# Norm factor after the projections: value tiles first, all projection tiles from unnormalised x, in a two-layer decoder trunk

## The reference

```python
def rms_norm(x, g):
    return x * rsqrt(mean(x * x, axis=-1, keepdims=True) + NORM_EPS) * g

def rope(x, pos):                      # on the first 16 of 64 channels of a head
    x1, x2 = x[..., :half], x[..., half:ROT_DIM]
    return concat([x1 * cos - x2 * sin, x2 * cos + x1 * sin, x[..., ROT_DIM:]])

h = rms_norm(x, norm_g) @ w_in         # one projection; split into q, k, v, gates ...
q_a, k_a, q_c, k_slc, k_win = rope(...)    # v and the raw rows of the compressed branch: no rope
x = x + merge_branches(p, o_a, o_b, o_c, w_up_a, w_up_b, w_up_c, w_out)
...
y = rms_norm(x, final_norm_g)
```

## Time and profile before

| | before |
|---|---|
| median of 3 runs | 1014.2 us (1012.84 to 1017.59) |
| profiled execution | 1013.01 us, of which the span of instructions is 1011.3 us |
| granted TensorE clock, mean over the span | 0.995 of full speed |
| PE busy | 948.9 us, 94% |
| DVE / ACT / POOL busy | 59% / 42% / 18% |
| HBM | 200.12 MB read, 40.18 MB written |

### The profile page before, as it was taken

How to read it: one execution, slowest core, us unless ns; L and a number is a source line. 1 busy time by engine, 2 the same in 40 slices (tenths; PEclk the granted TensorE clock), 3 DMA queues, 4 the chain that set the end, 5 groups by cost and what they waited for, 6 DMA issues and landing times. The chain is left out here.

```text
span 1011.3 us, 20944 instructions
## 1 busy us (share of the span) xinstructions
PE 948.9 (94%) x7828; PEld 864.0 (85%) x7836; DVE 597.5 (59%) x1305; ACT 424.3 (42%) x837; POOL 185.6 (18%) x320
## 2 busy tenths in 40 slices
PE   4999999998999999999999999999889999999995
PEld 4999887887778689999999998878777777999994
DVE  5868766557222357746686786665742234676564
ACT  5453345544312244334454434545432205443343
POOL 3010000126436620000000000003463464000000
PEclk9999999999999999999999999999999999999998
DMA  9563964536658881532645576636346699434421
GB/s 344 210 224 133 412 237 187 229 116 208 231 157 254 258 324 53 223 141 92 252 184 212 230 284 277 249 127 244 146 153 207 214 257 306 192 126 157 176 84 48
DMA packets 65189, 206.30 MB, mean 204 GB/s; under 512 B 12080, under 2 KB 49648, under 8 KB 55744
## 3 DMA queue, kind: packets, MB, share of 16 engines
q1 hardware_dynamic: 56048, 184.72, 49.3%
q0 software_dynamic: 8752, 19.63, 6.4%
q10 hardware_dynamic: 288, 0.60, 0.2%
HBM read 200.12 MB, written 40.18 MB: 238 GB/s over the span
## 5 line engine op out<-in xcount | busy, mean ns | idle before, releaser
L952 PE MATMUL bank<-xnT_high_r,paged_r 128*128 128x288 f32 x1088 | 327.7, 301 | 4.0 <-DVE oT_a L1687 2.4
L952 PE MATMUL bank<-xnT_r,paged_r 128*128 128x288 f32 x1024 | 302.7, 296 | 0.0
L952 PE MATMUL bank<-xnT_high_r,big_r 128*128 128x288 f32 x1024 | 301.8, 295 | 0.0
L1598 DVE TENSOR_TENSOR big_r<-big,paged_r 128x1024 fp32r<-128x1024 f32 x160 | 194.4, 1224 | 135.1 <-ACT paged_r L1399 134.4
L952 PEld LDWEIGHTS bank<-xnT_high_r,paged_r 128*128 128x128 f32 x1088 | 204.7, 188 | 11.6 <-issue 5.1
L952 PEld LDWEIGHTS bank<-xnT_high_r,big_r 128*128 128x128 f32 x1024 | 193.4, 189 | 0.0
L952 PEld LDWEIGHTS bank<-xnT_r,paged_r 128*128 128x128 f32 x1024 | 193.1, 189 | 0.0
L1399 ACT ACTIVATE paged_r<-big 128x1024 fp32r<-128x1024 f32 x160 | 166.4, 1050 | 7.4 <-DMA big<-in_w_feat 4.1
L1145 PE MATMUL bank<-paged,long 128*128 128x256 f32 x512 | 117.6, 383 | 2.1 <-DVE kvp L1773 1.7
L1145 PEld LDWEIGHTS bank<-paged,long 128*128 128x128 f32 x512 | 94.8, 190 | 19.8 <-issue 4.5
L922 POOL TENSOR_SCALAR short<-short,small 128x128 f32<-128x128 f32 (+1 forms) x64 | 50.6, 805 | 321.0 <-DVE small L1747 321.0
(11 more groups left out here) (294 smaller groups left out, 1473.7 us busy)
## 6 DMA issues: line engine op xcount, KB each, us to landing
big<-in_w_tok SPq DMA_DIRECT2D x13, 2048.0 KB, 8.5
big<-in_w_feat SPq DMA_DIRECT2D x12, 2048.0 KB, 8.6
big<-in_w_gate SPq DMA_DIRECT2D x10, 2048.0 KB, 8.6
out_kept_dil<-in_cache_dil SPq DMA_DIRECT2D x16, 1020.0 KB, 13.3
paged<-in_pool SPq DMA_DIRECT2D x218, 64.0 KB, 3.0
big<-in_w_up SPq DMA_DIRECT2D x12, 1024.0 KB, 8.8
paged<-in_pool POOLq DMA_DIRECT2D x166, 64.0 KB, 2.9
big<-in_kv_win SPq DMA_DIRECT2D x4, 2048.0 KB, 9.3
```

What stands on the lines that cost most here:

```text
L952: last = mm(out, l, r, start=(c == 0 and i == 0), stop=(c == n - 1 and i == 2))
L1598: v.tensor_tensor(l_part, full, h_part.bitcast(FP32), ALU.subtract).then_inc(*split_done.inc(s))
```

## The change

- The value tiles are projected first, then the keys; all 28 tiles read the unnormalised `xg`, so `RAW` and `pout` go. ACT evacuates all but the two cmp tiles, which DVE multiplies by `rnB`.
- The norm factor enters in three ways: in the rotation tables (`rots`: two DVE products of 128x288 into `rot_n`) for queries and keys, per token in the evacuation of the value transposes, and in `rnB` for the rest.
- `root` is now six PE products of one column, ones as the moving side, which leave the sum of squares as a column per token; ACT takes the square root of 128x3, DVE the reciprocal, and scales three pieces of the identity by it; `spread` multiplies ones by these diagonals, which gives the factor on every partition, and ACT copies it to `rnB`. In layer 0 `root` stands behind tile 3 and `spread` behind tile 4; in layer 1 behind tiles 0 and 1.
- Normalised x is still made, for the gate logits and the feature tiles; `norm` and `nlow` stand three tiles after `spread`, the last two chunks at tiles 13 to 15.
- The four value transposes move behind `gc`, and the rope of query type 3 (branch C) is split into two halves, on DVE behind the scaling of units 0 and 1. The zc feature tiles come before the za ones.
- In layer 0 the squares and their sums are POOL's, not ACT's and DVE's, and POOL's late constants are loaded behind them. ACT runs a square root on an unused tile at the head of each layer's start.
- The loads of the start: x in four parts, all on SP's queue, in the order x0, x1, w0, x2, x3, w1 to w3, constants, small loads.
- At the end the squares are made before the scaled x, the last square goes to PE unsummed, and `y` reads the factor from PSUM.

```diff
-TILES = [("k", t) for t in KEYED[0:4]] + [("v", t) for t in ("d1", "d4", "d16", "win")] + \
+TILES = [("v", t) for t in ("d1", "d4", "d16", "win")] + [("k", t) for t in KEYED[0:4]] + \
         [("k", "slc"), ("cmp", 0), ("cmp", 1), ("v", "slc")] + [("q", t, r) for t in range(4) for r in range(REP)]
 V_SLC = TILES.index(("v", "slc"))
-RAW = 8
-
-ROPES = {TILES.index(("k", "win")): ("k", 0), TILES.index(("k", "slc")): ("k", 1)} | \
+K_FIRST, K_SLC = TILES.index(("k", "d1")), TILES.index(("k", "slc"))
+
+ROPES = {TILES.index(("k", "win")): ("k", 0), K_SLC: ("k", 1)} | \
...
-FEATS = [("za", kt) for kt in range(WT)] + [("zc", kt) for kt in range(WT)] + \
+FEATS = [("zc", kt) for kt in range(WT)] + [("za", kt) for kt in range(WT)] + \
...
-        if i == 0:
-            out += [("root",), ("pout", 0)]
-        elif i == 1:
-            out += [("pout", 1), ("norm", 0), ("norm", 1)]
-        elif i == 2:
-            out += [("nlow", 0), ("nlow", 1), ("pout", 2), ("rnt",), ("norm", 2), ("norm", 3)]
-        elif i == 3:
-            out += [("nlow", 2), ("nlow", 3), ("pout", 3), ("norm", 4), ("norm", 5)]
-        elif i == 4:
-            out += [("nlow", 4), ("nlow", 5), ("norm", 6), ("norm", 7)]
-        elif i == 5:
-            out += [("nlow", 6), ("nlow", 7)]
-        elif i < 12:
+        root, first = (0, 1) if layer else (3, 4)
+        if i == root:
+            out.append(("root",))
+        elif i == first:
+            out += [("spread",), ("rots",), ("norm", 0), ("norm", 1)]
+        elif first < i < first + 3:
+            n = 2 * (i - first)
+            out += [("nlow", n - 2), ("nlow", n - 1), ("norm", n), ("norm", n + 1)]
+        elif i == first + 3:
+            out += [("nlow", 4), ("nlow", 5)]
+        elif 12 < i < 16:
+            out += [("nlow", z) for z in range(6, KT) if z == i - 8] + [("norm", z) for z in range(6, KT) if z == i - 7]
+        if i < 12:
...
+        if i in ROPES and ROPES[i] != ("q", 3):
             out.append(("rope",) + ROPES[i])
         if i == TILES.index(("cmp", 1)):
             out.append(("pairs",))
-        if RAW < i <= RAW + 3:
-            out.append(("vturn", i - RAW))
-        if i == V_SLC + 2:
-            out.append(("vturn", 0))
-    out += [("gc",), ("gct",)]
+    out += [("gc",)] + [("vturn", j) for j in range(4)] + [("gct",)]
...
+        if i < 2:
+            out.append(("rope", "q", 3, i))
...
-    out = start(0, 0) + halves(0, 0) + [s for i in range(1, KT) for s in start(0, i)] + halves(0, 1)
+    starts = [start(0, i) for i in range(KT)]
+    out = sum(starts[0:4], []) + halves(0, 0) + sum(starts[4:], []) + halves(0, 1)
...
-            out += [(layer, ("down", i // 4, i % 4))] + start(layer + 1, i)
+            out += [(layer, ("down", i // 4, i % 4))] + start(layer + 1, i)[::-1 if layer + 1 == DEPTH else 1]
...
-    return out + [(DEPTH, ("root",))] + [(DEPTH, ("y", i)) for i in range(KT // 2)]
+    return out + [(DEPTH, ("root",)), (DEPTH, ("spread",))] + [(DEPTH, ("y", i)) for i in range(KT // 2)]
...
+            load_x(0)
+            load_x(1)
+            load_first(0)
+            load_x(2)
+            load_x(3)
+            for q in range(1, 4):
+                load_first(q)
...
+                if k == "square" and layer == 0:
+                    i = s[1]
+                    pool.wait_ge(x_in[i // 2], 16)
+                    own = total[:, 0:T] if i == 0 else squared_x[i % 2][:, 0:T]
+                    done = nc.gpsimd.tensor_tensor(own, x[:, i, :], x[:, i, :], ALU.mult)
+                    if i == 0:
+                        done.then_inc(*summed.inc(s))
+                    elif i < KT - 1:
+                        link(done)
+                        pool.wait_ge(*summed.at(("square", i - 1)))
+                        nc.gpsimd.tensor_tensor(total[:, 0:T], total[:, 0:T], own, ALU.add).then_inc(*summed.inc(s))
+                    else:
+                        done.then_inc(*squared.inc(s))
+                        for dst, src in LATE:
+                            pool.dma_start(dst, src).then_inc(late_in, 16)
+                        numbers = page_numbers(pool, 0)
...
-                    pe.wait_ge(*summed.at(("square", KT - 1)))
-                    pe.wait_ge(set_up, 4)
+                    pe.wait_ge(*summed.at(("square", KT - 2)))
+                    pe.wait_ge(set_up, 6)
                     wait(pe, TR.is_free(s))
-                    mm(tr(s)[:, 0:T], ones[:, :], total, start=True, stop=True).then_inc(*TR.fill(s))
-                elif k == "rnt":
+                    for n, part in enumerate((total, squared_x[(KT - 1) % 2])):
+                        if n:
+                            pe.wait_ge(*squared.at(("square", KT - 1)))
+                        for tt in range(3):
+                            last = mm(tr(s)[:, tt:tt + 1], part[:, P * tt:P * (tt + 1)], ones[:, 0:1],
+                                      start=(n == 0 and tt == 0), stop=(n == 1), skip_group_check=True)
+                    last.then_inc(*TR.fill(s))
+                elif k == "spread":
                     pe.wait_ge(*inverted.at(("root",)))
                     pe.wait_ge(const_in, 16 * len(CONSTS))
-                    transposes(s, [(tr(s)[0:PARTS[tt], tt:tt + 1], rnB[0:1, TOK0[tt]:TOK0[tt] + PARTS[tt]])
-                                   for tt in range(3)])
+                    wait(pe, TR.is_free(s))
+                    for tt, n in enumerate(PARTS):
+                        last = mm(tr(s)[:, P * tt:P * tt + n], ones[0:n, :], diag[0:n, P * tt:P * tt + n],
+                                  start=True, stop=True, skip_group_check=True)
+                    last.then_inc(*TR.fill(s))
...
+                    precise(pj(s)[:, 0:T], lambda c: (wh[:, c, :], wl[:, c, :]),
+                            lambda c: (xg_high[:, c, :], xg_low[:, c, :]), KT, ("tok", g), q4,
+                            lambda c: x_split.at(("start", c))).then_inc(*PJ.fill(s))
                 elif k == "gc":
                     wait(pe, PJ.is_free(s))
                     pe.wait_ge(*layer_in.at("all"))
+                    pe.wait_ge(*xn_split.at(KT - 1))
...
+                    if i == 0:
+                        f(unused[:, layer:layer + 1], eps, ACT.Sqrt)
...
                 elif k == "root":
                     act.wait_ge(*TR.is_full(s))
-                    f(rnB, tr(s)[:, 0:T], ACT.Sqrt, bias=eps).then_inc(*TR.release(s))
-                elif k == "rnt":
+                    f(rn, tr(s)[:, 0:3], ACT.Sqrt, bias=eps, scale=1.0 / D_MODEL).then_inc(*TR.release(s))
+                elif k == "spread" and layer < DEPTH:
                     act.wait_ge(*TR.is_full(s))
-                    f(rn[:, 0:2], tr(s)[:, 0:2], ACT.Copy)
-                    f(rn[0:NS, 2:3], tr(s)[0:NS, 2:3], ACT.Copy).then_inc(*TR.release(s))
+                    f(rnB, tr(s)[:, 0:T], ACT.Copy).then_inc(*TR.release(s))
...
-                        f(v_prompt[:, :, slc], tr(s)[:, 0:2 * P].rearrange("p (t n) -> p t n", t=2), ACT.Copy)
-                        f(v_new[:, slc], tr(s)[0:NS, 2 * P:3 * P], ACT.Copy).then_inc(*TR.release(s))
+                        for tt, n in enumerate(PARTS):
+                            last = f(v_prompt[:, tt, slc] if tt < 2 else v_new[:, slc], tr(s)[0:n, P * tt:P * (tt + 1)],
+                                     ACT.Identity, scale=rn[0:n, tt:tt + 1])
+                        last.then_inc(*TR.release(s))
...
-                    v.reciprocal(rnB, rnB).then_inc(*inverted.inc(s))
-                    dve.wait_ge(*inverted.at(s))
-                elif k == "pout":
-                    dve.wait_ge(*PJ.is_full(("proj", s[1])))
-                    v.tensor_tensor(raw[0][:, s[1], :], pj(("proj", s[1]))[:, 0:T], rnB, ALU.mult)\
-                        .then_inc(*PJ.release(("proj", s[1])))
+                    link(v.reciprocal(rn, rn))
+                    if layer == 0:
+                        dve.wait_ge(const_in, 16 * len(CONSTS))
+                    for tt, n in enumerate(PARTS):
+                        last = v.tensor_scalar(diag[0:n, P * tt:P * tt + n], ident[0:n, 0:n], rn[0:n, tt:tt + 1], None,
+                                               ALU.mult)
+                    last.then_inc(*inverted.inc(s))
+                elif k == "rots":
+                    dve.wait_ge(*TR.is_used(("spread",)))
+                    v.tensor_tensor(rot_n[:, 0, :], rot_c[:, :], rnB, ALU.mult)
+                    link(v.tensor_tensor(rot_n[:, 1, :], rot_s[:, :], rnB, ALU.mult))
+                elif k == "proj" and TILES[s[1]][0] == "cmp":
+                    dve.wait_ge(*PJ.is_full(s))
+                    v.tensor_tensor(raw_cmp[:, TILES[s[1]][1], :], pj(s)[:, 0:T], rnB, ALU.mult).then_inc(*PJ.release(s))
```

152 lines of the change are left out of this document (80 added, 72 removed).

## The result

| | before | changed | changed, run again |
|---|---|---|---|
| median | 1015.55 us | 1020.33 us | 1022.73 us (before beside it: 1014.19) |
| ratio to before, 95% interval | | 1.0046 (1.0025 to 1.0067) | 1.0079 (1.0058 to 1.0101) |
| span of the profiled execution | 1011.3 us | 1017.5 us | 1021.8 us |
| granted clock, mean | 0.995 | 0.996 | 0.991 |

What follows compares the result with a forecast made beforehand. TensorE (PE), busy 94% of the span, was taken as the bound. Six parts, -2.3 + 2.5 - 0.3 + 1.3 + 4.4 - 2.7 = +2.9 us, gave 1016.5 us; range 1006 to 1024.

Steps and rivals of the forecast that it cites:

- part 5: Last query rope as two DVE halves among the first score units: extra PE waits, +4.4 us net (0 to +9.9).
- part 1: Start to tile 7: earlier first product, new root products, squares on POOL; -2.3 us (ends -5.5 and +2.2).
- Rival C: Layer 0 root: last sum on POOL ends 5 us late, PE stands behind tile 3; 1020.5 us, chance 0.08.
- E: Start: loads compete as before, first product stays at 11.9; 1019.5 us, chance 0.05.
- Rope of the keys: Behind tile 7: rope waits for its evacuation, PE waits at tile 10; +2.5 us (0 to +4).
- Layer 1's root: Layer 1's start: new root and spread products without a gap replace product, wait and transposes; -0.3 us (-1.8 to +0.2).
- Transposes: Value transposes leave the projections and lengthen the tail before the first score; net +1.3 us (-3.1 to +3).
- End: Last tile to y: preloaded table and shorter reciprocal, less new scalings and products; -2.7 us (-3.4 to -1.5).
- Rival B: Key rope, tail and query halves all swallowed by DVE and ScalarE gaps; 1006.6 us, chance 0.22.
- Rival D: First three score units: both waits full in both layers, clock falls; sign: score u3 waits over 3 us; 1023.7, chance 0.15.

Runs made afterwards that it cites:

- e10: The changed kernel with POOL's late constants (the masks among them) issued ahead of layer 0's squares, not behind them; 1021.13 us, ratio to before 1.0075.
- e2: The changed kernel with the four key tiles first and the value tiles as tiles 4 to 7; ratio to before 1.0079.
- e5: The changed kernel with the edits of e1 and e2 together; 1010.23 us, ratio to before 0.9963.
- e11: e5 with layer 0's last pair of low parts of normalised x behind the rope of the keys, not ahead; 1009.07 us, ratio to before 0.9954.
- e1: The changed kernel with the last query rope whole again, on DVE right behind the last projection tile; 1010.42 us, ratio to before 0.9974.
- e4: The changed kernel without the early square root on an unused tile in the final stage; 1021.55 us, ratio to before 1.0084.
- e8: The changed kernel with the first rope half behind the gates' sums in DVE's queue, the second unchanged; 1021.35 us, ratio to before 1.0074.

## Why the prediction was right, and where it was not

The time fell inside the range, and the forecast of no change that can be told, or a little slower, came out at the slower edge: +4.8 us in the medians, or 0.46%, just inside the 0.5% that the prediction had set itself, and 0.79% when run again, outside it. The two profiles are 6.2 apart; without the fall of the clock at 632, which the second profile of the changed kernel doesn't have, the parts below come to +4.6, where the sum said +2.9. That the miss isn't larger is partly luck: part 5 cost 1.6 more than forecast, and part 1 gave 0.8 more, for reasons that the forecast didn't have.

1. **Start.** Forecast -2.3, measured 25.79 + 15.09 against 31.21 + 12.80: -3.1, and from -3.6 to -2.3 by the profiles with the same start. Two errors, of which one hid the other. The first product is at 10.13 and not 9.2: ACT could round the first quarter at 7.59, where the sum had it landed at 6.8, and its split took 1.40, not 1.23. From there to tile 3's end it is 15.66 us, forecast 15.6. And the 1.7 us set aside for POOL and DVE were not needed, but for the 0.17 of that split. The sums on POOL were not late at all: 14 instructions in 15.3 us, over at 19.4, wanted at 25.6. A square takes 0.67 alone, not the 1.04 drawn from scalings of another form. DVE lost more time than the 0.7 us that I gave it (the earlier trace rows shows POOL slowed and no price for DVE, but four splits of x take 3.70 in place of 1.80), yet off the path: it waited for ACT's rounding all the same. The Trainium skill ("SBUF — State Buffer", Who interferes with whom) says that a DVE instruction with two SBUF inputs contends with a GpSimd instruction that reads SBUF, and that whichever issues first blocks the other. The trace agrees in that both engines' instructions grew (0.67 to 1.68 on POOL, 1.23 to 2.12 on DVE); it does not bear out the consequence drawn from it, that this part would come out near zero. Rival C fell, and E too; e10 shows that my reason against E was the wrong one, since the first quarter lands as early with the masks beside it. They do slow the quarters behind it. The small products of the root cost 2.29, forecast 2.15.
2. **Rope of the keys.** Forecast +2.5; the wait at tile 10 is there in both layers, and against a cadence of 12.80 it is 1.38 and 1.36, together +2.7. e2 confirms the cause in layer 1, where the keys first give 1.18 back. In layer 0 they give 0.35; the rest is the norm's work in DVE's queue, which lets the rope start 0.85 later against the landmark than in layer 1 (e5). e11 was meant to test this and could not. The forecast had 1.5 and 1.0 for the two layers, so the sum fits better than its parts.
3. **Layer 1's root.** Forecast -0.3, measured -0.35.
4. **Transposes.** In the projections 0.82 + 0.75 = 1.57 a layer are saved, forecast 1.55. In the tail the first score stands 5.75 us behind the last tile's landmark (603.07 to 608.82), before 3.30 (602.09 to 605.39): 2.45 longer, forecast 2.2.
5. **Halves of the last rope.** This is the term that was mis-sized. Forecast +4.4, net of the tail; undisturbed, attention in layer 1 grew by 51.32 - 45.25 = 6.07, without the tail's 2.45 3.6, and in layer 0 by 4.8, without it 2.4, since the kernel before had its fall of the clock there: +6.0, and +7.5 in the first profile with the fall at 632. The mechanism and the first wait were as written (1.65 forecast, 1.71 measured). Each half took DVE 3.41 us, forecast 3.2. The 3.3 at score u3 came as 1.40 at the split and 1.68 at the score. The step that failed is what was to be given back: the 0.85 of the wait on L1554. It is 1.24 at 651.35 as it was at 642.79, and 1.12 in the second profile, where the clock did not fall ahead of it; from score u3 to that score PE takes 17.07 us before and 17.06 in the second profile. So the delay moved DVE and PE alike. e1 shows the whole term to be a matter of place: 9 us of idle DVE stood open one step earlier. I had priced the halves against the old place of the rope, and never asked what the old place would now cost: with the longer tail, nothing: e1's attention is 0.9 us longer than the old one (46.16 against 45.25), and the tail alone is 2.45 longer.
6. **End.** Forecast -2.7, measured 52.98 - 55.41 = -2.4. e4 puts 1.26 on the preloaded table, 0.82 by itself and 0.44 behind PE's longer stop, where the clock was lower. In the kernel before the load started behind PE's products ([1.38 <-PE bank L975] before it, at 1001.87), so there nothing of its 1.28 was hidden. The Trainium skill ("ScalarE: Activation LUTs", What ACT_TABLE_LOAD costs) adds a drain of about 1.38 us to a switch of tables. It isn't in this trace: the load in e4 starts 0.02 us behind ACT's last instruction and the square root right behind the load.

Rival B fell: no wait of parts 2, 4 and 5 was swallowed. Rival D was right that the waits would come in full in both layers, 4.8 us each, and wrong that nothing would be given back: the 1.2 on the first feature tile was. Its sign, over 3 us at score u3, didn't come (1.68), and the clock fell behind it in one of the two profiles (+1.5 us), not always. e8 gives the sharper case: after a stop of 3.17 us it fell in both layers.

## What to carry to other kernels

Before an edit moves a long instruction group into a queue, list that engine's idle spans in the new order, not the old one: here the old place of the rope (5.9 us of DVE), widened by the longer tail, stood open as 9 us of idle DVE, and whole and in that place the rope cost PE no wait (e1). Work moved between two engines that slow each other, as DVE and POOL do here, must be priced on both; take the row in which both run, and then ask whether either was on the path at all. And where a median can't tell, intervals between landmarks tell a few tenths of a microsecond, if they hold no fall of the clock and don't start with a load that has to land: the first interval here moved by 1.3 us between kernels with the same start. Before an edit is taken as a test, check in its trace that what it moved has passed the instruction that is waited for; e11's had not.

## What was not expected of the hardware

- POOL's square of 288 columns takes 0.67 us alone, 0.88 beside the short splits on DVE and up to 1.68 beside the long ones; four short splits on DVE take 3.70 beside POOL's sums and 1.80 without them (e10), a weight split up to 2.12 (e10) against 1.23.
- The granted clock falls to its lower level (1.2 of 2.4 GHz) for some microseconds, and costs 1.3 to 2.8 us each time. After a 3.17 us stop of PE it fell in both layers; after stops of 1.4 and 1.7 (at 632) and of 2.7 (at 249) it fell in one run and not in another of the same kernel.
